# Sample retention between the halves of the first compression product, and the encoding bias computed in four column groups

## Time and profile before

| | |
|---|---|
| runs | 2968.64, 2970.62, 2973.92 us |
| median | 2970.62 us |
| the profiled execution | 2970.14 us |
| its span | 2968.4 us |
| mean granted clock of TensorE | 0.93 |
| busy share of TensorE, DVE, ACT, POOL | 92%, 32%, 21%, 16% |

### The profile page before, as it was taken

The page is one execution under the profiler, slowest core; times in us unless marked ns, Lnnn a source line. Parts: engine busy times, 40 slices in busy tenths (PEclk is TensorE's granted clock), DMA queues, the critical chain, the costliest instruction groups (busy, mean ns, idle before and its releaser), DMA issues.

```text
span 2968.4 us, 44563 instructions
## 1 busy us (share of the span) xinstructions
PE 2723.0 (92%) x18210; PEld 2239.0 (75%) x18210; DVE 936.4 (32%) x2658; ACT 636.7 (21%) x1613; POOL 484.8 (16%) x465
## 2 busy tenths in 40 slices
PE   7999994998989777995799999999999999999995
PEld 3555543744666556552799999999999999999995
DVE  1121221323766522245322222222232232223221
ACT  1111111113756500121011111111111111111111
POOL 0000002101000000022123222222232332122121
PEclk9989995898999966897899999999999999999997
DMA  5000018303000111322677778797898999998995
GB/s 185 11 22 13 20 56 197 65 4 112 1 1 1 54 59 58 107 80 90 248 248 248 268 258 297 259 309 273 302 303 314 321 321 315 330 320 306 316 327 169
DMA packets 276720, 533.63 MB, mean 180 GB/s; under 512 B 51858, under 2 KB 88178, under 8 KB 276306
## 3 DMA queue, kind: packets, MB, share of 16 engines
q1 hardware_dynamic: 223794, 472.66, 44.8%
q0 software_dynamic: 33312, 46.98, 7.4%
q10 hardware_dynamic: 19408, 11.10, 1.4%
HBM read 492.21 MB, written 42.96 MB: 180 GB/s over the span
## 4 chain that ended last, share of the span: by engine, by line
PE 51%; DMA 1%; DVE 1%; SPq 0%; POOL 0%; issue 0%; POOLq 0%; DVEq 0%; ACT 0%; ACTq 0%
PE up L2046 34%; PE down L2057 17%; DMA w_up<-summed_rows 1%; DMA slot_rows<-slot_tokens_gates 0%; DMA summed_rows<-y_rows,row_index_cur 0%; SPq L1994 0%; POOL summed_rows L2010 0%; PE down L2063 0%; POOLq L1890 0%; DVE nb L2178 0%; DVE hT L2135 0%; DVEq L1955 0%; DVE obt L2184 0%; DVE obt L2189 0%; DVE start L2171 0%
## 5 line engine op out<-in xcount | busy, mean ns | idle before, releaser
L2046 PE MATMUL up<-hT,w_up 128*128 128x128 f32 (+19 forms) x8192 | 1008.0, 286 | 18.2 <-DVE hT L2135 18.2
L2046 PEld LDWEIGHTS up<-hT,w_up 128*128 128x128 f32 x8192 | 1004.9, 191 | 18.5 <-issue 18.5
L2057 PE MATMUL down<-actT,w_down 128*128 128x128 f32 (+19 forms) x4096 | 507.8, 286 | 0.0
L2057 PEld LDWEIGHTS down<-actT,w_down 128*128 128x128 f32 x4096 | 503.6, 191 | 1.1
L2010 POOL DMA_INDIRECT summed_rows<-y_rows,row_index_cur x153 | 240.9, 1574 | 1085.4 <-ACT y_rows L2076 1048.8
L2155 DVE TENSOR_SCALAR glu<-up,b_up_cur 128x128 f32<-128x128 f32 (+19 forms) x256 | 93.6, 366 | 1019.4 <-PE up L2046 1019.4
L306 PE MATMUL zp<-w_in,xnT 128*128 128x512 f32 (+3 forms) x896 | 368.0, 567 | 1.4 <-DVE xnT L480 1.4
L306 PEld LDWEIGHTS zp<-w_in,xnT 128*128 128x128 f32 (+1 forms) x896 | 157.7, 192 | 186.6 <-issue 182.7
L2087 ACT ACTIVATE sig<-glu 128x128 f32<-128x128 f32 (+19 forms) x256 | 82.4, 322 | 868.4 <-DVE glu L2155 868.4
L2095 ACT ACTIVATE yT<-down,b_down_cur 128x128 f32<-128x128 f32 (+19 forms) x256 | 97.1, 379 | 394.5 <-PE down L2057 394.5
L2004 POOL DMA_INDIRECT x_rows<-h_rows,row_index_cur x153 | 149.7, 978 | 65.3 <-issue 46.0
(11 more groups left out here) (391 smaller groups left out, 2088.7 us busy)
## 6 DMA issues: line engine op xcount, KB each, us to landing
w_up<-in_w_up SPq DMA_DIRECT2D x128, 2048.0 KB, 12.7
w_down<-in_w_down SPq DMA_DIRECT2D x64, 2048.0 KB, 12.6
w_in<-in_w_in SPq DMA_DIRECT2D x5, 2048.0 KB, 13.4
cache_rows<-in_cache_slc_kv SPq DMA_DIRECT2D x40, 128.0 KB, 3.0
x<-in_x_prompt SPq DMA_DIRECT2D x8, 512.0 KB, 3.5
window_rows<-in_cache_win_kv SPq DMA_DIRECT2D x8, 512.0 KB, 4.3
window_rows<-in_x_prompt SPq DMA_DIRECT2D x8, 512.0 KB, 3.6
summed_rows<-rg SPq DMA_DIRECT2D x8, 512.0 KB, 2.6
```

Source lines behind the costliest of these rows:

```text
L2046: mm = nc.tensor.matmul(up[c % 2][:, h, :N], U[c // 4][:, h, kk, w0:w0 + P], hT[:, kk, :N], start=(kk == 0), stop=(kk == KC - 1))
L2057: mm = nc.tensor.matmul(dn[d % 2][:, :N], Dn[:, kk // 4, kk % 4, d * P:d * P + P], aT[:, kk, :N], start=(kk == 0), stop=(kk == KC - 1))
```

## The change

- The retention outputs (`ret_o`) go to two of the three transpose banks and the scores (`ret_s`) to `kcp` and `vcp`, so `cacc` is no longer used by the retention; `qx` and `sTm` move from the tile for values to an unused part of the tile for keys.
- TensorE: `retention()` is called between the first and the second half of M(0,k). It also waits for the evictions of the two banks. T(1,k) waits for DVE's copy of the outputs (`s_rc`), and the wait for the updated state moves from ahead of the key bias to S(source,k).
- The encoding bias: 16 matmuls for keys and 16 for values with 256 columns of w1 moving and one column of the encoding, broadcast to 32 columns, as weights. Matmul jj writes to partitions 32*(jj % 4) and on, so four partial sums of 4 matmuls each, each repeated on 32 partitions. DVE copies the 128x256 result to SBUF; behind the product's first half, two matmuls with a moving column of 1/32 sum over the 128 partitions, and DVE copies the bias.
- DVE: `sample_operands()` moves from the front to behind the copy of the key bias parts, `sample_state()` behind the copy of the key bias. A memset of the 1/32 column is added. DVE's `link` behind the oret copies becomes an increment of `s_rc`.

The diff, cut to its core:

```diff
+        of_k = xT[0][:].rearrange("p b g n -> p (b g n)")
+        qx = of_k[:, 1024 + NT * 256:1536 + NT * 256].rearrange("p (i b n) -> p i b n", i=2, b=DB)
...
+        share = sb("one_32nd", [P, 1])
...
-        ret_s = [t[:SR, 0:2 * SR].rearrange("p (i n) -> p i n", i=2) for t in acc]
-        ret_o = [t[:SR, 128:128 + 2 * HD].rearrange("p (i n) -> p i n", i=2) for t in acc]
-        kcp, vcp, bp = ps("kcp", [P, 512]), ps("vcp", [P, 512]), ps("cbp", [P, 4])
+        ret_o = [t[:SR, 0, :].rearrange("p (i n) -> p i n", i=2) for t in tp[1:]]
+        kcp, vcp, bp = ps("kcp", [P, 512]), ps("vcp", [P, 512]), ps("cbp", [P, 512])
...
         ret_d = [kcp, vcp]
+        ret_s = [t[:SR, 0:2 * SR].rearrange("p (i n) -> p i n", i=2) for t in ret_d]
+        s_bp, s_rc = sem("pe_bias_parts_copied"), sem("s_ret_out_copied")
...
                 pe.wait_ge(s_rm, 1)
+                for e in range(2):
+                    pe.wait_ge(s_te[e], done_by(3, e))
...
                 if op == "T":
+                    if (gi, kv) == (1, 0):
+                        pe.wait_ge(s_rc, 1)
...
-                    if (gi, kv) == (0, 0):
-                        retention()
                 if op == "M":
                     if gi == 0:
                         pe.wait_ge(s_w[kv], 32)
-                        if kv == 0:
-                            pe.wait_ge(s_st, 1)
-                        for hh in range(2):
-                            for jj in range(16):
-                                mm = nc.tensor.matmul(bp[:, 2 * kv + hh:2 * kv + hh + 1], w1[kv][:, jj, hh * P:hh * P + P],
-                                                      pe_c[:, kv, jj:jj + 1], start=(jj == 0), stop=(jj == 15))
+                        if kv:
+                            pe.wait_ge(s_be, 1)
+                        for jj in range(16):
+                            q = 32 * (jj % 4)
+                            mm = nc.tensor.matmul(bp[q:q + 32, HID * kv:HID * kv + HID], pe_c[:, kv, jj:jj + 1].broadcast_to([P, 32]),
+                                                  w1[kv][:, jj, :], start=jj < 4, stop=jj >= 12)
                         mm.then_inc(s_b, 1)
...
                         mm.then_inc(s_m, 1)
+                        if gi == 0 and hh == 0:
+                            pe.wait_ge(s_bp, kv + 1)
+                            for part in range(2):
+                                mm = nc.tensor.matmul(bp[:, HID * kv + part:HID * kv + part + 1], sq_r[:, part * P:part * P + P], share[:],
+                                                      start=True, stop=True)
+                            mm.then_inc(s_b, 1)
+                            if kv == 0:
+                                retention()
...
                     if kv == 0:
+                        pe.wait_ge(s_st, 1)
...
-                link(last)
+                last.then_inc(s_rc, 1)
...
-            sample_operands()
+            nc.vector.memset(share[:], 1.0 / 32)
...
-                if (op, gi, kv) == ("M", 0, 0):
-                    sample_state()
...
                 if op == "M" and gi == 0:
-                    dve.wait_ge(s_b, kv + 1)
-                    nc.vector.tensor_copy(bias[:, 2 * kv:2 * kv + 2], bp[:, 2 * kv:2 * kv + 2]).then_inc(s_be, 1)
+                    dve.wait_ge(s_b, 2 * kv + 1)
+                    nc.vector.tensor_copy(sq_r[:], bp[:, HID * kv:HID * kv + HID]).then_inc(s_bp, 1)
+                    if kv == 0:
+                        sample_operands()
+                    dve.wait_ge(s_b, 2 * kv + 2)
+                    nc.vector.tensor_copy(bias[:, 2 * kv:2 * kv + 2], bp[:, HID * kv:HID * kv + 2]).then_inc(s_be, 1)
+                    if kv == 0:
+                        sample_state()
```

More of the change, by code:

```diff
@@ L583, in phase_compress @@
         of_v = xT[1][:].rearrange("p b g n -> p (b g n)")
-        qx = of_v[:, 0:512].rearrange("p (i b n) -> p i b n", i=2, b=DB)
-        sTm = of_v[:SR, 512:512 + 4 * SR].rearrange("p (h n) -> p h n", h=4)
+        of_k = xT[0][:].rearrange("p b g n -> p (b g n)")
+        qx = of_k[:, 1024 + NT * 256:1536 + NT * 256].rearrange("p (i b n) -> p i b n", i=2, b=DB)
+        sTm = of_k[:SR, 1536 + NT * 256:1536 + NT * 256 + 4 * SR].rearrange("p (h n) -> p h n", h=4)
         vz = of_v[:SR, 1024:3072].rearrange("p (h b d) -> p h b d", h=4, b=DB)
@@ L839, in sample_operands, with turned @@
                 nc.vector.tensor_tensor(so[:, 1], ret_s[1][:], dm[:, 1], ALU.mult).then_inc(s_rm, 1)
+            def turned(gi, kv):
+                for m in range(nT(gi)):
+                    n = first_t[gi, kv] + m
+                    if n % 2 == 0:
+                        dve.wait_ge(s_t, n + 1)
+                        if gi == 1 and kv == 1:
+                            dve.wait_ge(s_out, 32)
+                        if gi >= 1:
+                            dve.wait_ge(s_m, first_m[gi - 1, kv] + 2)
+                        nc.vector.tensor_copy(by_phase(xT[kv][:, m // G, m % G, :]), in_order(tp[n % 3])).then_inc(s_te[0], 1)
             def sample_state():
@@ L889, in _ @@
                 if op == "T":
[L890 to L898, removed]
-                if op == "M" and gi == 0:
-                    dve.wait_ge(s_b, kv + 1)
-                    nc.vector.tensor_copy(bias[:, 2 * kv:2 * kv + 2], bp[:, 2 * kv:2 * kv + 2]).then_inc(s_be, 1)
+                    turned(gi, kv)
+                if op == "M" and gi == 0:
+                    dve.wait_ge(s_b, 2 * kv + 1)
[6 more added lines that the diff above has]
+                        sample_state()
                 if op == "S" and kv == 0:
```

## The result

The changed kernel takes 2956.75 us (median of five, 2949.67 to 2958.29) for 2970.62; the ratio is 0.9949, interval 0.9935 to 0.9963. The forecast was 2955.5, between 2950.0 and 2961.5.

A forecast was written before the change was run, and what follows sets the result against it. TensorE, busy for 92% of the span, was taken to set the compression phase's time. Value side 11.3 plus key side 3.7 gave 15.0 us off the profiled 2970.14: 2955.1, stated as 2955.5, range 2950 to 2961.5.

The forecast's parts named there:

- The total: Whole kernel: 15.0 us gained, all in the compression phase, for a forecast time of 2955.5 us.
- Value side: From the end of S(0,k) to the end of M(0,v): 9.8 us instead of 21.1, a gain of 11.3.
- Rival A: New value bias: column groups run in a row, 6.9 us instead of 1.9; total gain 10.0, 2960.5 us; chance 0.09.
- Rival B: Clock low at the value bias: bias 3.6 us, M(0,v) low 5.7 us; gain 10.6, 2960 us; chance 0.06.
- Rival D: New biases: each record waits for the whole one before, value bias 21.4 us; slower, some 2978 us; chance 0.03.
- The rule of the Trainium skill on weight loads: New biases: loads overlap matmuls only on another row group, so each round shows its load; value bias 2.7 us, not 1.9.
- Key side: Up to T(1,k): M(0,k) starts at ACT's first eviction, T(1,k)'s first eviction follows gates() at 533.3 for 537.07; gain 3.7 us.
- 12.4 us as before (...), and I take off 0.9: Retention between M(0,k)'s halves: stays at the half clock, less 0.9 us because the clock has just risen.
- the forecast's upper bound of 6.4: Key side's largest gain, 6.4 us: retention at full clock, with the pages' landing at 530 us as the limit.
- So nothing takes the gain back: Phases after compression: they start at barriers with loads issued relative to them, so they give back nothing of 15.0 us.
- Rival C: M(0,k) split: first half's clock lost in the retention; if all low, key side gains 0.7, 2958.5 us; chance 0.05.

The follow-up runs named there:

- second profile: The changed kernel run again with no edit: median 2954.84 us, 0.9941 of the kernel before; compression 221.5 us, prompt attention 341.5.
- the run ahead: Against the changed kernel, the retention moved ahead of M(0,k)'s first half, its outputs in cacc: median 2948.19 us, 0.9917 of the kernel before.

## Why the prediction was right or wrong

- **The total** was right, 2955.5 for 2956.75 and 2954.84, but as the sum of two errors: compression gained 18 to 19.6 us for the 15.0 forecast, and the prompt attention gave back 4.4 that the forecast had as nothing. That the two errors nearly cancel is luck.
- **Value side: right.** 11.3 forecast, 11.3 measured (21.06 to 9.72). Four groups side by side, 1.93 us for 1.9; M(0,v) at the full clock, two halves of 3.84 and 3.82 for 7.4; the sum 0.51 for 0.46. Rival A is out: one group alone takes 7.09 and costs about 5 us. Rival B is out: the clock is 1.00 from 528 to 537.8. Rival D is out: the records follow at 0.215 us even on one group. The rule of the Trainium skill on weight loads (page "TensorE: Matmul & The Clock Gate", section "Part 3: Packing small matmuls — row/col tiling"), by which I had made 2.7 us of the bias, does not hold in this case: the trace shows the loads wholly beside matmuls of the same rows.
- **Key side: its events right, one term wrong.** The first half starts behind ACT's eviction (41.8 us after the phase's start, 42.0 forecast) and T(1,k)'s first eviction right behind gates(). The step that failed is the retention's duration: "12.4 us as before (...), and I take off 0.9". It was 6.85 us in the first profile and 9.2 in the second. I had read 0.50 through the whole retention in rows 3 as a property of its small matmuls. Behind an idle time they did stay there (again 12.4 us in the run ahead), but behind the first half the clock they find is full, and they keep it for a while. Of the seven profiles with the retention between the halves, two kept it to the retention's end (6.85 us), and in five it fell 4.2 to 5.8 us into it (7.8 to 9.2 us); why in these and not in those stays open. The second half was 3.84 and 6.39 us, where I took 5.7. Gain 7.4 to 8.0 for 3.7; it lies beyond the forecast's upper bound of 6.4, which rested on the pages' landing, 63 us after the phase's start. In the changed kernel ACT's page issues ended 55.8 us after it, not 59.9, and T(1,k) started at 58.2 without waiting for a DMA.
- **"So nothing takes the gain back": wrong.** Later phases do start at barriers, their loads are relative to them, but the clock's changes are not. The delay runs show it: 2.3 us more in front of the barrier changed the next phase by about -5.7 us in one kernel and +4.9 in the other. I had the spread of runs as the only uncertainty behind the phase.
- **Rival C** came true in one half: in five of those seven profiles the clock of the first half was lost in the retention, and the second half behind it ran low at first (6.39 us in the changed kernel's second profile). But its price took the retention itself at the half clock too, which it mostly was not: even in that profile the key side gained 7.4 us, where rival C had 0.7. Behind both halves the phase was 4.4 to 6.1 us longer than between them.

## What to carry to other kernels

A product with one moving column pays a full 128x128 weight load a record and lets the clock fall for what follows; with the operands exchanged and the result spread over the four column groups the same sum took 1.93 us, and 0.51 to add the parts, for 11.06. Work of small matmuls was cheaper behind dense work (6.85 to 9.2 us) than behind an idle time (12.4). That is a price and no rule for its place: put into an idle time that was there anyway, the dear 12.4 us let M(0,k) end 3.3 to 7.4 us earlier, and the median of that kernel is the lowest here. A gain is counted to the next late event only, found by asking which engine's own queue (here ACT's 37 us of DMA issue) stands in front of it; and a few microseconds gained in one phase can cost or bring as many in the next by the clock alone, so compare phases, not spans.

## What the runs showed of the hardware that was not expected

- The same retention records took 12.4 us at 0.50 behind an idle time and 6.85 at 1.00 behind 5.4 and 5.7 us of 128x128 products with 126 columns; in five other profiles the clock fell within them (7.8 to 9.2 us).
- One, two and four column groups: 7.09, 3.65, 1.93 us for 32 float32 records of 256 columns; 0.215 us a round at the full clock, and 3.64 us for four groups at the half clock.
- A phase of 337 us with unchanged instructions has two lengths, 335.5 to 337.3 and 340.4 to 341.8 us, according to where the clock's fall next to its start lies (1.1 to 2.2 us from it, or within 0.5 and once 2.8 us); a delay of 2.3 us switched it in both directions.
